# Two blocks of a transformer on one core: the order of products in groups of three weight tiles, the roundings at the first norm, and fewer products with constants

## The reference

```python
def _modulate(x, shift, scale):
    return _layernorm(x) * (1.0 + scale) + shift

def _post(x, f, gate, g, b):
    return _layernorm(ALPHA * x + gate * f, g, b)

def _ffn(h, p):
    return (jax.nn.silu(h @ p['w_ff_gate']) * (h @ p['w_ff_up'])) @ p['w_ff_down']
...
    a, b = jnp.split(c, 2, axis=-1)          # second block: c is a convolution of h @ w_up
    return (jax.nn.silu(a) * b) @ w_down
```

## Time and profile before

| | us |
|---|---|
| median of 3 runs | 3046.82 |
| lowest, highest run | 3043.12, 3053.45 |
| profiled execution | 3046.38 |
| its span, first to last instruction | 3044.6 |
| PE busy | 2846.8 (94%) |
| POOL, ACT, DVE busy | 1380.8, 1323.3, 1301.1 |
| mean granted TensorE clock | 0.969 |

### The profile page before, as it was taken

How to read it: one execution, slowest core, us unless ns; L and a number is a source line. 1 busy time by engine, 2 the same in 40 slices (tenths; PEclk the granted TensorE clock), 3 DMA queues, 4 the chain that set the end, 5 groups by cost and what they waited for, 6 DMA issues and landing times.

```text
span 3044.6 us, 45194 instructions
## 1 busy us (share of the span) xinstructions
PE 2846.8 (94%) x18910; PEld 2445.1 (80%) x18910; DVE 1301.1 (43%) x2725; ACT 1323.3 (43%) x2220; POOL 1380.8 (45%) x646
## 2 busy tenths in 40 slices
PE   7999998899999999998999899899898899898898
PEld 5778876688876888877788699899886799777897
DVE  3777766532234111015677653322246441163440
ACT  3254443323424232225454346444455564444563
POOL 3432030244432543436423177588651588522785
PEclk9999999999999999999999999999999899898899
DMA  6332022133324343334211154356542355331354
GB/s 235 119 104 81 29 83 75 43 123 92 118 85 161 124 144 124 112 128 166 91 49 49 36 167 152 112 168 181 150 132 98 102 182 170 120 132 56 128 180 122
DMA packets 103554, 359.48 MB, mean 118 GB/s; under 512 B 11126, under 2 KB 17526, under 8 KB 102840
## 3 DMA queue, kind: packets, MB, share of 16 engines
q1 hardware_dynamic: 103352, 356.60, 36.5%
HBM read 355.51 MB, written 1.05 MB: 117 GB/s over the span
## 4 chain that ended last, share of the span: by engine, by line
PE 81%; DVE 9%; ACT 6%; POOL 2%; issue 1%; DMA 1%; SPq 0%; DVEq 0%; ACTq 0%
PE PS L357 80%; DVE AR L1773 2%; ACT AR L1141 2%; DVE PS L1781 1%; POOL RINGL L2490 1%; ACT WH L1121 1%; ACT XT L1141 1%; DVE XT L1773 1%; DVE AR L1781 1%; PE PS L368 1%; ACT L1141 1%; DVE SM L2007 1%; DVE AR L1934 1%; DVE AR L1777 0%; POOL HTR L2495 0%
## 5 line engine op out<-in xcount | busy, mean ns | idle before, releaser
L2490 POOL TENSOR_TENSOR RINGL<-RING,WH 128x1024 fp32r<-128x1024 f32 (+1 forms) x554 | 1299.1, 2357 | 1549.0 <-ACT WH L1121 1548.3
L357 PE MATMUL PS<-HTR,WH 128*128 128x256 f32 (+2 forms) x2736 | 876.6, 321 | 0.0
L1121 ACT ACTIVATE WH<-RING 128x1024 fp32r<-128x1024 f32 (+1 forms) x554 | 568.2, 1034 | 655.0 <-PE PS L357 525.3
L357 PE MATMUL PS<-HTH,WH 128*128 128x256 f32 (+1 forms) x2336 | 750.0, 322 | 30.4 <-POOL RINGL L2490 24.0
L357 PE MATMUL PS<-HTH,RINGL 128*128 128x256 f32 (+1 forms) x2336 | 724.8, 316 | 1.8 <-POOL RINGL L2490 1.8
L357 PE MATMUL PS<-ARR,WH 128*128 128x256 f32 (+2 forms) x2688 | 692.8, 325 | 18.0 <-ACT WH L1121 5.8
L357 PEld LDWEIGHTS PS<-HTR,WH 128*128 128x128 f32 (+1 forms) x2736 | 524.8, 192 | 39.9 <-issue 2.1
L357 PEld LDWEIGHTS PS<-ARR,WH 128*128 128x128 f32 (+1 forms) x2688 | 468.0, 191 | 64.7 <-issue 14.6
L357 PEld LDWEIGHTS PS<-HTH,WH 128*128 128x128 f32 x2336 | 450.0, 193 | 72.1 <-issue 34.0
L357 PEld LDWEIGHTS PS<-HTH,RINGL 128*128 128x128 f32 x2336 | 443.3, 192 | 30.7 <-POOL RINGL L2490 2.7
L357 PE MATMUL PS<-ARR,RINGL 128*128 128x256 f32 (+1 forms) x1472 | 466.3, 327 | 1.5 <-POOL RINGL L2490 1.5
(11 more groups left out here) (195 smaller groups left out, 3366.8 us busy)
## 6 DMA issues: line engine op xcount, KB each, us to landing
RING<-w_ada_in SPq DMA_DIRECT2D x96, 512.0 KB, 3.7
RING<-w_up_in SPq DMA_DIRECT2D x88, 512.0 KB, 3.4
RING<-w_gates_in SPq DMA_DIRECT2D x48, 512.0 KB, 3.6
RING<-w_ff_gate_in SPq DMA_DIRECT2D x44, 512.0 KB, 3.7
RING<-w_ff_up_in SPq DMA_DIRECT2D x44, 512.0 KB, 3.7
RING<-w_glu_in SPq DMA_DIRECT2D x32, 512.0 KB, 4.5
RING<-w_ff_down_in SPq DMA_DIRECT2D x32, 512.0 KB, 3.5
RING<-w_in_in SPq DMA_DIRECT2D x32, 512.0 KB, 3.6
```

The costliest lines, as they stand in the source:

```text
L357: return e.matmul(out_, lhsT, rhs, start=start, stop=stop)
L1121: e.activation(RINGS[name][:, j, 0:width], RING[:, b % NSLOT, 0:width], ACT.Copy).then_inc(*a_upper.up(b))
L2490: e.tensor_tensor(RINGL[:, i, 0:width], RING[:, i, 0:width], RINGS[name][:, j, 0:width], ALU.subtract).then_inc(*g_lower.up(b))
```

## The change

`group` takes one more argument, `ready_hi`, the signal of the inputs' upper parts. For each slice, PE now waits for the upper part of the inputs, does the upper-with-upper products of the three blocks, then waits for the lower part, and does the three upper-with-lower products; before, it waited for the lower part at once and did the six in pairs. The wait for a block's rounding (`a_upper`), which stood in `load` for all three blocks ahead of the first product, now stands ahead of each product with that block. The products, their number and the sums are the same. At the first norm, ACT rounds one weight block ahead of the slices instead of three, and one more after each of slices 0 and 1. The constants' products are 10 instead of 18 at the first norm, 6 instead of 9 ahead of the first feed-forward part, and 5 instead of 7 at the two others.

```diff
--- before.py
+++ after.py
@@ -386,8 +386,6 @@
                 blocks.append((src, width, name, j, same[-size] if len(same) >= size else None))
                 if lower:
                     pe.wait_ge(*g_lower.to(n))
-                else:
-                    pe.wait_ge(*a_upper.to(n))
                 return n, RINGS[name][:, j, :], RINGL[:, n % NSLOT, :]
 
             def project(name, l, ct, src, ready, cols, until, kt_total=8, order=range(8)):
@@ -408,7 +406,7 @@
                 p_block.also(name, l, ct)
                 stage_block[name, l, ct] = n
 
-            def group(l, items, src, ready, cols):
+            def group(l, items, src, ready_hi, ready, cols):
 
                 hi, lo = src
                 work = []
@@ -416,9 +414,12 @@
                     o = take(name, l, ct, until=until)[:, 0:cols.stop - cols.start]
                     work.append((name, ct, o, *load(A[name][l, ct, :, 0:1024], 1024, lower=False)))
                 for k in range(8):
+                    pe.wait_ge(*ready_hi(k))
+                    for name, ct, o, n, up, low in work:
+                        pe.wait_ge(*a_upper.to(n))
+                        mm(o, up[:, k * P:k * P + P], hi(k, cols), k == 0, False)
                     pe.wait_ge(*ready(k))
                     for name, ct, o, n, up, low in work:
-                        mm(o, up[:, k * P:k * P + P], hi(k, cols), k == 0, False)
                         mm(o, up[:, k * P:k * P + P], lo(k, cols), False, False)
                 for name, ct, o, n, up, low in work:
                     pe.wait_ge(*g_lower.to(n))
@@ -518,7 +519,7 @@
                 pe.wait_ge(*d_norm.to("rstd", *nid))
                 out_of_strips(o, RSTD, n).then_inc(*p_norm.up("rstd", *nid))
                 if nid[0] == "m" and nid[1:] != (0, 1):
-                    hum(9 if nid == ("m", 0, 2) else 7)
+                    hum(6 if nid == ("m", 0, 2) else 5)
 
             def gla_gates(l, seq, tile):
                 for d in range(2):
@@ -815,12 +816,12 @@
                     fill_all()
                     ring("WH0")
                     ada_at[:] = 4, 4, 12
-                    hum(18)
+                    hum(10)
                 h0 = lambda k: g_norm.to("lo", *part(("m", l, 1), k, 0 if l else 1))
                 h1 = lambda k: g_norm.to("lo", "m", l, 1, k)
                 halves = [("w_glu", i % 2 * 8 + i // 2, (a_merge if i % 2 else d_merge, "glu", l, i // 2))
                           for i in range(16)]
-                group(l, halves[0:3], HA, h0, cols)
+                group(l, halves[0:3], HA, lambda k: a_norm.to("hi", *part(("m", l, 1), k, 0 if l else 1)), h0, cols)
                 for name, ct, until in halves[3:]:
                     project(name, l, ct, HA, h0, cols, until)
                 fill(1)
@@ -849,7 +850,7 @@
                     fill_all()
                 merge(l, 2, "w_conv_o", CP, h2, lambda k: d_conv.to("cp", l, k))
                 group(l, [("w_out", ct, (a_merge, "res", l, "w_out", ct)) for ct in range(3)], MP,
-                      lambda k: d_merge.to("mp", l, k), cols)
+                      lambda k: a_merge.to("mp", l, k), lambda k: d_merge.to("mp", l, k), cols)
                 for ct in range(3, 8):
                     residual(l, "w_out", ct, MP, lambda k: d_merge.to("mp", l, k), 8)
                 if not last:
@@ -858,7 +859,8 @@
                 layernorm(("m", l, 2), XT, lambda k: pe.wait_ge(*a_norm.to("post", l, 1, k)), cols)
                 h3 = lambda k: g_norm.to("lo", "m", l, 2, k)
                 group(l, (("w_ff_gate", 0, (a_ffn, "gate", l, 0)), ("w_ff_up", 0, (d_ffn, "ff", l, 0)),
-                          ("w_ff_gate", 1, (a_ffn, "gate", l, 1))), HB, h3, cols)
+                          ("w_ff_gate", 1, (a_ffn, "gate", l, 1))), HB, lambda k: a_norm.to("hi", "m", l, 2, k), h3,
+                      cols)
                 for j in range(1, NFF):
                     if j > 1:
                         project("w_ff_gate", l, j, HB, h3, cols, (a_ffn, "gate", l, j))
@@ -1097,7 +1099,7 @@
                 h = lambda k: g_norm.to("nlo", l, 2, k)
                 halves = [("w_up", i % 2 * NFF + i // 2, (d_ffn, "conv", l, i % 2 * NFF + i // 2))
                           for i in range(2 * NFF)]
-                group(l, halves[0:3], HN, h, X)
+                group(l, halves[0:3], HN, lambda k: a_norm.to("nhi", l, 2, k), h, X)
                 for name, ct, until in halves[3:]:
                     project(name, l, ct, HN, h, X, until)
                 mix_out(l, "w_down", FP2, lambda k: d_ffn.to("lo2", l, k), NFF, 14336)
@@ -1121,10 +1123,10 @@
                     e.activation(RINGS[name][:, j, 0:width], RING[:, b % NSLOT, 0:width], ACT.Copy).then_inc(
                         *a_upper.up(b))
 
-            def phase(i):
+            def phase(i, n=3):
                 up_at[0] = phases[i][0]
                 up_end[0] = phases[i + 1][0] if i + 1 < len(phases) else len(blocks)
-                uppers(up_at[0] + 2)
+                uppers(up_at[0] + n - 1)
 
             def ahead(*label):
 
@@ -1192,6 +1194,8 @@
                 p, c = norm_parts(nid, cols)[0]
                 for k in range(8):
                     modulate_tile(nid, p, c, k, shift, scale, upper)
+                    if nid == ("m", 0, 1) and k < 2:
+                        uppers(up_at[0])
 
             def modulate_tile(nid, p, c, k, shift, scale, upper):
                 l = nid[1]
@@ -1528,7 +1532,7 @@
                 last = l == DEPTH - 1
                 cols = cols_of(l)
                 if l == 0:
-                    modulate(("m", 0, 1), BOTH, 0, 1, HA[0], none, lambda: phase(0))
+                    modulate(("m", 0, 1), BOTH, 0, 1, HA[0], none, lambda: phase(0, 1))
                     ada_at[:] = 4, 4, 12
                 glu(l)
                 fill(1)
```

## The result

| us | before | after |
|---|---|---|
| median of 20 runs each | 3046.93 | 3052.02 |
| lowest, highest | 3043.12, 3053.45 | 3048.81, 3056.12 |
| profiled execution, its span | 3046.38, 3044.6 | 3051.18, 3049.4 |

The ratio is 1.0015, with a 95% interval of 1.0009 to 1.0021: within the 0.3% that I had set as no change, and yet clear of none. The changed kernel is 5.1 us slower. I had 3047.0, 0.2 above before; 3052.02 lies 0.02 us beyond the end of my range. That the time stays within 0.3% came true, but 0.3% is 9.1 us here: the width of that band made it true, not the sum of +0.4. One execution of before, among those beside the last four experiments, took 12028 us and is left out of every number.

The account below looks back on a forecast made before the run. PE, busy for 94% of the span, was taken as the bound. The terms +2.3 - 0.45 - 0.24 - 0.5 - 0.7 = +0.4 us put the profiled execution at 3046.8; the forecast median was 3047.0, range 3042 to 3052.

Parts of the forecast that it names:

- first norm, `w_glu` of layer 0: PE waits for the third block's rounding, +0.85 us, and the clock falls behind it, +1.5: +2.3 in all.
- `w_out`, layer 0: Two products of 0.23 us done in PE's wait for the third block's rounding: -0.45 us.
- `w_out`, layer 1: Two products of 0.12 us done in PE's wait for the third block's rounding: -0.24 us.
- feed-forward group, layer 0: Three products done ahead of the first lower part, 0.69 us, some 0.2 lost to POOL: -0.5 us.
- `w_glu` and feed-forward groups, layer 1: POOL's chain sets the time and PE waits for it whatever it starts with: 0.
- `w_up`, twice: PE starts 0.8 us sooner, 3 more products fall in the low clock, -0.36 us each: -0.7 together.
- POOL taking back 0.2 us of the 0.69: Layer 0's feed-forward group: PE's 0.69 us lead meets POOL's lower part for the next block; some 0.2 lost.
- The numbers of products don't change, so the reordering itself costs nothing; only starts and the clock move: All groups: with the same products, the new order has no cost of its own, 0.
- three fewer free nothing: Layer 0's feed-forward group: constants ended ahead of the upper part, so removing three gains nothing; clock expected to hold.
- the first norm costs nothing or gains: Rival: no clock fall there, sum -1.1 us (3045.7); PE also never waiting, -3.8 (3043.0); chance 0.2.
- That POOL takes the gains: Rival, each group: PE's lead ends at a weight's lower part, leaving only +2.3 us (3049.1); chance 0.16.
- The other side, whole groups at the low clock (3065): Rival: first-norm and layer 0 feed-forward groups wholly slow, +9.7 us each; chance 0.03; one or two short falls 0.06.

Follow-up runs that it names:

- the last four experiments: The third batch of experiments, on another chip than the other batches, with the kernel before beside it: median 3045.86 us (34 runs).
- e7: Kernel before with only the roundings at the first norm in turn with the slices; all three blocks awaited ahead of the first product: 3047.88 us, ratio 1.0010.
- e1: Kernel before with only the fewer constants' products (10 for 18, 6 for 9, 5 for 7 twice): 3049.35 us, ratio 1.0006.
- e3: Changed kernel with the roundings at the first norm as before (three blocks ahead of the slices): 3047.93 us, ratio 0.9999 to before.
- e2: Changed kernel with the constants' products of before (18, 9, 7, 7): 3049.88 us, ratio 1.0011 to before.
- e4: Kernel before with only the new order in the groups and its single waits; constants and roundings as before: 3046.47 us, ratio 0.9998.
- e8: Changed kernel with 8 more constants' products just ahead of the first norm's wait for the third block: 3049.81 us, ratio 1.0009 to before.
- e11: Changed kernel with constants of before and, at the first norm, two blocks rounded ahead, the third after slice 0: 3047.69 us, ratio 1.0006 to before.
- e12: Kernel before with the third weight block rounded three times at the first norm, so that inputs come 2.2 us later: 3050.78 us, ratio 1.0013.
- e9: Kernel before with only the new order and single waits, the same kernel as e4, on another chip: 3047.92 us, ratio 1.0008.
- e5: Kernel before with 10 for 18 constants' products at the first norm alone: 3048.58 us, ratio 1.0008.
- e6: Kernel before with fewer constants' products at the three later norms alone (6 for 9, 5 for 7 twice): 3048.23 us, ratio 1.0013.
- e9 to 11: Includes, between e9 and e11, kernel before with new order and more later-norm constants (12 for 9, 10 for 7 twice): 3046.45 us, ratio 1.0004.

## Why the prediction was right or wrong

**Right, term by term at the places.** Against the start of each place, in the two profiles:

| term | predicted | measured |
|---|---|---|
| first norm, `w_glu` of layer 0 | +2.3 | +2.4 |
| `w_out`, layer 0 | -0.45 | -0.45 |
| `w_out`, layer 1 | -0.24 | -0.24 to -1.8 |
| feed-forward group, layer 0 | -0.5 | -0.5 |
| `w_glu` and feed-forward groups, layer 1 | 0 | 0 |
| `w_up`, twice | -0.7 | -0.27, -0.15 |
| sum | +0.4 | +0.8 |

(`w_out` of layer 0: ACT's third rounding came 3.71 us later than before, 893.66 to 897.37, and its rounding behind the group 3.26 later. The feed-forward group: POOL's start 3.67 later, 981.58 to 985.25, and the next block's first product 3.18 later. Layer 1: POOL's start and the fourth block 2.70 and 2.69 later. For `w_out` in layer 1 the place itself was 1.8 us shorter, for a low stretch at 1932.3 in before is gone; it is not the change's, and the sum counts 0.24.) All this is one profiled pair; the runs can't show terms this small. And one part was luck: I took the clock to fall at the first norm, and it did in this execution, but it held behind 2.71 us in e7 and behind 2.93 us in e1. The step of the order of ACT's list, the wait for the third block, POOL taking back 0.2 us of the 0.69, and POOL's chains in layer 1 all came as written. In the `w_up` groups only the size was off: 0.56 us of an 0.85 us earlier start went back to the low clock.

**Wrong: what the clock does away from the places.** The step that failed is the sentence "The numbers of products don't change, so the reordering itself costs nothing; only starts and the clock move", together with "three fewer free nothing": I moved the clock in one place alone and left it as it was in the rest of 3000 us. Of the 4.8 us between the two spans, the places make 0.8 and a later start 0.4; 3.6 us came in stretches where both kernels have the same instructions. PE was busy for 150.9 us of after's low stretches and for 143.3 us of before's: 7.6 us more, and since a product takes nearly twice as long there, at most 3.8 us of time, places included. And the median lies another 0.8 us above the execution profiled.

How much is clock? An estimate from the runs: over the 100 of the kernel before, the time falls by 2.2 us (± 0.15) for each 0.001 of mean clock. (Within all the other kernels: 1.9 ± 0.1.) From before's mean of 0.9692 to after's of 0.9670 that is 4.2 to 4.7 us. The means over all runs, 3046.60 and 3052.26, differ by 5.7. The upper bound, if PE had been busy in every low microsecond: 0.0022 less of clock over 3049 us is half of 13.4 us more at the low level, 6.7 us. The places without their clock part (+0.85 - 0.45 - 0.24 - 0.5 - 0.4 = -0.7) and 4.2 to 6.7 of clock give 3.5 to 6.0, which holds what was measured. So, by this estimate, the change's direct effect was a small gain and its effect through the clock took 4 to 6 us. That the clock went down with the change is measured; that it made the loss is argued from this slope and from the low stretches, and no run held the clock fixed.

Which edit does it? With the new order in place, the roundings in turn cost 4.8 ± 1.0 us (after less e3) and 4.8 ± 1.1 (e2 less e4), of which the place itself shows 3.3 and 1.6; without the order 2.4 ± 1.2 (e7). The fewer constants cost 0.8 to 0.9, with errors of 1.0 and 1.1, on top of the order (e3 less e4, after less e2), and 2.3 ± 1.0 without it (e1); the order alone +0.9 ± 0.7. The roundings in turn are the one part that costs clear of noise in the changed kernel; e8, e11 and e12 point to the hole that they open ahead of the first group.

**Where it is the change's, and where it is chance.** The low stretches up to about 1500 us differ between two executions of one kernel (e4 and e9). The end does less so: from ACT's 361st weight rounding on (2209.2 us in before; the 363rd in e12, which has two more), there are four patterns; the first two below repeat to 0.1 and 0.3 us. Starts and lengths of the first low stretches from that rounding on:

```
before, e5, e6, e7, e12:     (105.4, 3.4) (129.3, 3.4) (177.1, 17.1) ...             low 108.8 us, to the end 835.4
after, e2, e3, e4, e9 to 11: (17.4, 3.4) (106.1, 3.4) (130.0, 3.4) (160.8, 6.8) ...  low 112.8 us, to the end 836.7 to 837.0
e8:                          the same up to the one at 532.7, then fewer             low 106.4 us, to the end 833.8
e1:                          the same up to the one at 181.3, then others            low 112.1 us, to the end 836.1
```

All seven executions of the second row have the new order, and each is 1.3 to 1.6 us longer there than before, where I had promised -0.7. But e8 has the order too and is 1.6 us shorter than before, and e1 has the low stretch at 17.4 without it. So the order goes with the slower pattern in seven executions of eight; it does not fix it, and that this loss is the order's own is not shown. Why the stretch at 17.4, a good 170 us ahead of the first `w_up` group, comes up is not settled.

**The rivals.** That the first norm costs nothing or gains: it cost 2.4, though e3 and e4, with three roundings ahead, had it 1.0 and 0.9 us shorter than before. That POOL takes the gains: it did not, beyond the 0.2 us foreseen. The other side, whole groups at the low clock (3065): no group stayed low. It had the right subject, though; the clock took its share in many pieces, most of 3.4 us, spread over the kernel, each far from 9.7 us, and not in two groups. Its chance for short falls stood at 0.06, for one place. A case "mean clock down by 0.002, +4 us" was missing.

The Trainium skill, page "SBUF — State Buffer", section "SBUF: two separate sides", was weighed in the prediction; the experiments show it better than before's trace did. In 13 of the 14 executions DVE's small operation on `MOD` began while POOL's weight operation ran, and took 2.00 to 2.29 us. In e4 it ended just ahead of it (DVE's row, then POOL's):

```profile
41.58 0.17 DVE L1779 TENSOR_SCALAR MOD<-MOD 128x8 f32<-128x8 f32 x1
...
41.78 2.37 POOL L2492 TENSOR_TENSOR RINGL<-RING,WH 128x1024 fp32r<-128x1024 f32 x1 [41.34 <-ACT WH L1123]
```

It took 0.17 us. The inputs still did not come sooner there, since ACT had the third weight block, late from DMA, until 44.4.

**A version that beats before?** None. The order alone, with the roundings as before, is -0.5 in one batch and +2.3 in the other; with more constants +0.9. All are within what these runs tell from no change. The roundings of before are the better ones; for its constants the runs speak less clearly.

## What to carry to other kernels

In a kernel that keeps TensorE over 90% busy, cost an idle hole ahead of large products at its length and, as a case with a chance of its own, a slow stretch behind it (here some 1.4 us where the clock fell). Don't take a filler that ends ahead of the inputs as free to remove: ask what it does for the clock. Sum the places for the sign of a change, and then put the spread of the mean clock (here 0.001 is about 2 us, an estimate from the runs) on top as a case of its own, with more chance on the loss when the change opens holes. One profiled execution shows one phase of the clock: before reading a stretch as "slow because of X", look at it in a second execution of the same kernel.

## What the runs showed of the hardware that I had not expected

- The length of a hole in PE's work doesn't settle what the clock does behind it. It held behind 2.93 us (e1, first norm), 2.71 (e7) and 2.33 (e6, feed-forward group); it fell behind 2.32 (e1, the same group as in e6) and behind after's 1.60, which had another 0.27 just ahead of it.
- Two profiled executions of one kernel had 184.5 and 201.6 us at the low clock. The Trainium skill, page "TensorE: Matmul & The Clock Gate", section "Part 1: The HAM clock gate (the "warmup" mystery)", says that the gate's watch runs freely and isn't reset by a kernel's start. The traces agree: within each of the 14 executions all low stretches, from the first to the last, start on one even beat, to 6 ns, and where the beat lies against the first instruction differs from one execution to the next.
- By the last 835 us the work has fallen into step with that beat. The beat next after the 361st rounding comes 0.25 to 0.52 us behind it in nine executions and 2.96 to 2.99 us behind it in the five that have before's pattern, and nowhere else. Why only at these two places is not shown.
- 36 instructions of constants took 4.26 us at full clock and 5.89 us when a slow stretch fell on them, so whether they end ahead of the inputs at the first norm (e4) or hide their wait (before, e2, e9) changes from one execution to the next.
